# The recurrent mixer's triangular solve: 64x64 products replaced by products of the 32x32 blocks that are used

## What is computed

```python
def wkv_scan(s0, scan_in):
    def step(s, inp):
        w, kk, a, k, v, r = inp
        sa = jnp.einsum('dbhij,dbhj->dbhi', s, kk)
        s = s * w[..., None, :] - sa[..., :, None] * (kk * a)[..., None, :] + v[..., :, None] * k[..., None, :]
        return s, jnp.einsum('dbhij,dbhj->dbhi', s, r)
    return lax.scan(step, s0, scan_in)
```

## Time and profile before

| | us |
|---|---|
| median of 3 runs | 4448.5 (4442.09 to 4452.32) |
| the profiled execution | 4456.09 |
| its span | 4454.4 |
| busy in the span: PE, PEld, DVE | 3987.5, 2850.2, 2761.6 |
| busy in the span: ACT, POOL | 1455.8, 903.2 |
| granted TensorE clock, mean | 0.967 |
| the mixer's phase, from the span's start | about 2092 to 2822 |

### The profile page before, as it was taken

How to read it: one execution, slowest core, us unless ns; L and a number is a source line. 1 busy time by engine, 2 the same in 40 slices (tenths; PEclk the granted TensorE clock), 3 DMA queues, 4 the chain that set the end, 5 groups by cost and what they waited for, 6 DMA issues and landing times. The chain is left out here.

```text
span 4454.4 us, 75524 instructions
## 1 busy us (share of the span) xinstructions
PE 3987.5 (90%) x29982; PEld 2850.2 (64%) x29982; DVE 2761.6 (62%) x5967; ACT 1455.8 (33%) x3250; POOL 903.2 (20%) x926
## 2 busy tenths in 40 slices
PE   8989999988999899998999999898999777777777
PEld 6747887756788687787888888686444333333332
DVE  5674433665533476755666666235778888888885
ACT  3353342343523335712444544333111111111111
POOL 1101110110201101110000000100344444444443
PEclk9999999999999999998999999899999999999999
DMA  4203443311443310231000000434999999999998
GB/s 130 82 26 111 155 139 98 105 33 38 158 148 121 116 57 20 73 124 47 19 18 26 24 18 6 140 112 153 378 405 421 421 416 413 413 406 416 414 407 336
DMA packets 150673, 795.25 MB, mean 179 GB/s; under 512 B 19960, under 2 KB 23272, under 8 KB 83504
## 3 DMA queue, kind: packets, MB, share of 16 engines
q0 software_dynamic: 84560, 574.75, 32.0%
q1 hardware_dynamic: 58272, 188.32, 13.0%
q10 hardware_dynamic: 7488, 27.30, 1.9%
HBM read 766.11 MB, written 20.00 MB: 176 GB/s over the span
## 5 line engine op out<-in xcount | busy, mean ns | idle before, releaser
L3228 PE MATMUL psum<-rows,diag 128*128 128x512 f32 x2048 | 967.2, 620 | 260.2 <-ACT diag L3107 247.4
L3228 PEld LDWEIGHTS psum<-rows,diag 128*128 128x128 f32 x2048 | 396.1, 198 | 788.6 <-issue 775.6
L2926 POOL DMA_INDIRECT rows<-in_peer_uv,sel_idx x512 | 616.0, 1203 | 739.7 <-PE psum L3228 682.7
L2969 DVE SCALAR_TENSOR_TENSOR uh<-rows,h_rows 128x1024 f32<-128x1024 f32 x512 | 627.8, 1226 | 208.9 <-DMA rows<-in_peer_uv,sel_idx 183.1
L529 DVE TENSOR_TENSOR w_split_lo<-w_raw,w_split_hi 128x1024 fp32r<-128x1024 f32 (+1 forms) x271 | 327.2, 1218 | 496.1 <-ACT w_split_hi L516 491.4
L516 ACT CAST w_split_hi<-w_raw 128x1024 fp32r<-128x1024 f32 (+1 forms) x271 | 276.6, 1028 | 613.7 <-PE psum L465 395.0
L3100 ACT ACTIVATE g<-g 128x4 f32<-128x4 f32 x128 | 26.3, 205 | 1087.8 <-DVE g L2980 1087.8
L693 POOL TENSOR_TENSOR uT_lo<-normed_rows,uT_hi 128x512 fp32r<-128x512 f32 x64 | 90.3, 1411 | 667.0 <-ACT uT_hi L669 667.0
L465 PE MATMUL psum<-hT_mlp_hi,w_split_hi 128*128 128x512 f32 x512 | 201.7, 394 | 5.2 <-DVE hT_mlp_lo L261 5.1
L465 PE MATMUL psum<-hT_mlp_lo,w_split_hi 128*128 128x512 f32 x512 | 201.0, 393 | 0.0
L465 PE MATMUL psum<-hT_mlp_hi,w_split_lo 128*128 128x512 f32 x512 | 200.8, 392 | 0.0
(11 more groups left out here) (528 smaller groups left out, 8505.8 us busy)
## 6 DMA issues: line engine op xcount, KB each, us to landing
w_raw<-in_w_in SPq DMA_DIRECT2D x105, 512.0 KB
w_raw<-in_w_up SPq DMA_DIRECT2D x64, 512.0 KB
w_raw<-in_w_down SPq DMA_DIRECT2D x64, 512.0 KB
amask_sb<-in_w_mod ACTq DMA_DIRECT2D x48, 512.0 KB, 4.6
wq<-in_peer_wq SPq DMA_DIRECT2D x24, 512.0 KB
rows<-in_peer_uv,sel_idx POOLq DMA_INDIRECT x512
qkpad<-in_w_out SPq DMA_DIRECT2D x12, 512.0 KB, 5.5
w_raw<-in_w_out SPq DMA_DIRECT2D x12, 512.0 KB
```

Of the source, the lines that this page charges most:

```text
L2926: nc.gpsimd.indirect_dma_start(out=rows[:, n % RB, :], out_offset=None, in_=I["peer_uv"], in_offset=bass.IndirectOffsetOnAxis(ap=sel[:, t, ...
L2969: nc.vector.scalar_tensor_tensor(prod[:], rows[:, n % RB, 0:D], 1.0, h[:, t, :], ALU.mult, ALU.mult, accum_out=dots[:, (n // BATCH) % 2, s ...
L3228: last = nc.tensor.matmul(psum[:, 2 * (t % 2) + half, :], diag[:, n % (2 * BATCH), :], rows[:, n % RB, D + half * NB:D + (half + 1) * NB], ...
```

## The change

It replaces `by_head` in the 30 solve groups of each unit. Levels 1 to 4 use `by_quarter`: for each of the four quarters of the partitions, the 32x32 product of the head's diagonal block on those partitions. Level 5 uses `across`: for each head one 32x32 product, from one quarter's rows to the other quarter's output partitions. The rest of a cell's PSUM region and of U isn't written any more. All other products, waits, copies and masks are as they were.

```diff
+    quarters = tuple(slice(32 * j, 32 * j + 32) for j in range(4))
...
+    def by_quarter(out, lhsT, rhs):
+
+        for j, at in enumerate(quarters):
+            own = quarters[j % 2]
+            last = nc.tensor.matmul(out[at, own], lhsT[at, own], rhs[at, own], start=True, stop=True)
+        return last
+
+    def across(out, lhsT, rhs, source, target, mine, others):
+
+        for h in range(2):
+            rows = quarters[2 * h + source]
+            last = nc.tensor.matmul(out[quarters[2 * h + target], others], lhsT[rows, mine], rhs[rows, others],
+                                    start=True, stop=True)
         return last
...
                     for i in range(4):
                         c = 4 * b + i
-                        last = by_head(psum[:, b, i * L_CH:(i + 1) * L_CH], AT[:, c], X[:, c], True, True)
+                        out = psum[:, b, i * L_CH:(i + 1) * L_CH]
+                        if lv < LEVELS:
+                            last = by_quarter(out, AT[:, c], X[:, c])
+                        else:
+                            last = across(out, AT[:, c], X[:, c], d, 1 - d, quarters[1 - d], quarters[d])
                     last.then_inc(u_ready, 1)
...
                         y = Y[:, u % 3, c]
-                        l_, r_ = (y, U[:, c]) if lv < LEVELS else (U[:, c], y)
-                        last = by_head(psum[:, b, i * L_CH:(i + 1) * L_CH], l_, r_, True, True)
+                        out = psum[:, b, i * L_CH:(i + 1) * L_CH]
+                        if lv < LEVELS:
+                            last = by_quarter(out, y, U[:, c])
+                        else:
+                            last = across(out, U[:, c], y, 1 - d, d, quarters[d], quarters[1 - d])
                     last.then_inc(z_ready, 1)
```

## The result

The changed kernel takes 4502.35 us (median of 4, 4497.29 to 4512.57) against 4448.5 for the kernel before beside it (median of 3, 4442.09 to 4452.32): a ratio of 1.0126, interval 1.0111 to 1.014. A fourth execution of the kernel before, slow at 5680.36 us, is left out of its median. The change costs about 54 us, where 18 were forecast (4467): the sign and the range hold, the size is short by 35 us.

A forecast was written before the change was run, and what follows sets the result against it. TensorE's order of issue was taken to bound the mixer's phase. Stream and shape changes summed to +8 us (10.7 - 2.5), clock +10, together nearly +19 on the 4448.5 median: 4467 us, range 4442 to 4550.

The forecast's parts named there:

- the sign: Whole kernel: slower by over 0.2%, given 0.74; faster by over 0.2% and within it, 0.13 each.
- the range: Whole kernel: 4442 to 4550 us, with 2 in 10 left outside.
- What bounds the phase: Mixer's phase, 730 us: TensorE's order of issue sets its length, not the solve's own chain.
- The stream: Solve groups: four 32x32 products side by side take 32 ns, a group 0.254 us instead of 0.467; 102 us saved.
- The rival of four that don't start together: Solve groups: only two products stream side by side, 4565 us, or issue bounds each record, about 4725; chance 0.09 together.
- The change of shape: Between 64x64 and 32x32 groups: 0.095 us each way, plus next weights loaded in the open, 0.025 entering, 0.05 leaving.
- the W slots: Solve groups between W's products and N's, covering a wait: loss of only +0.01 us each; full loss would add 5 us.
- The longer program, "which I cost at nothing": Instruction fetch for levels 1 to 4, whose instructions double: costed at nothing, as DMA engines are 7% busy.
- the estimate of the sequencer's speed: TensorE's feed: 24 instructions shown under 8 ns each, up to 88 wanted in 0.9 us; near but enough.
- The clock: Mixer's phase: sparse stretches fall to 1.2 GHz in every second iteration, 8 more at 1.3 us, +10 us.
- The prediction's own sign of being wrong: Mixer's slices: a clock under 0.95 would show the forecast wrong.
- Iteration 0: No scan there, so solve follows solve without a change of shape from slot 12: shorter, -2.5 us taken between 0 and 4.5.

The follow-up runs named there:

- half_quarters: Changed kernel with levels 1 to 4 multiplying only quarters 0 and 2, half of the blocks left out; 4539.41 us, ratio 1.0204 to the kernel before.
- level5_only: Kernel before with only level 5 (96 of 480 solve groups) in 32x32, levels 1 to 4 unchanged; 4455.65 us, ratio 1.0009.

## Why the prediction was right, and where it was short

- **What bounds the phase** held: TensorE's order of issue. All of the change's effects were read from its starts.
- **The stream** held: four 32x32 products run side by side, 32 ns a set, and an undisturbed group of 32 matmuls takes 262 ns from first to last start. The rival of four that don't start together falls for the pitch, 8 ns for each matmul. The 25 ns per matmul of the Trainium skill, "TensorE: Matmul & The Clock Gate", Back-to-back issue gap, doesn't hold across tiles here.
- **The change of shape** held as a price, 0.10 us from start to start for 64x64 to 32x32, with the weights in the open behind it. Its sum was set too high. For units 1 to 14 it gave +9.5 us; the line through `half_quarters` leaves 14 x 0.08 = 1 (standard error 2.4). `level5_only` costs 0.10 to 0.15 us in six of its eight units at full clock and gains 0.12 and 0.17 in the other two, where the prices give 0.2 to 0.3 of loss. Perhaps more of the visits lie in front of a wait than the W slots counted; that was not tried.
- **The longer program, "which I cost at nothing"**, is the step that failed. It was argued from a DMA share of 7%, which says nothing on how fast one queue's blocks follow each other; and the estimate of the sequencer's speed (10 ns an instruction wanted, 8 shown over 24) was about a short run of instructions, not a supply over microseconds. Dry time in the phase rose by 24 us, 20 of them in units 1 to 14: where a slot wants an instruction every 10 ns, the supply gave one in about 14.
- **The clock** was the right mechanism and mis-sized: 8 stretches and 10 us expected, 62 us more of low clock found, which at 0.36 to 0.44 is 22 to 27 us. The prediction's own sign of being wrong, a clock under 0.95 in the mixer, came: 0.93. The reason given (the groups stream half as long) is not the whole of it. `half_quarters` streams as long as the changed kernel, with half of the products at work, and has twice the low clock.

For units 1 to 14 together: they are 46.2 us longer than before. 68 us more low clock x 0.36 = 24.6; dry time +20; together 44.6, leaving 1.6 for stream and shape. At 0.44 the clock has 30, and the sum is 4 us over; so the clock took 25 to 30, the supply 20, stream and shape about nothing. Iteration 0 was not shorter either (39.7 us, 39.1 before): 4.4 us more of low clock and two dry places of 0.7 and 0.8 us stand against what it saved.

The range held in part by luck. It was wide because of the clock, and some 24 of the 54 us came from the supply, which had no term in it. The phase took 776 us, outside the 740 to 755 that the prediction named. The sign rested on +8 for shape and stream, which came out near nothing, and on the clock, which was right. Dry time and low clock are not quite separate, since a dry place also lets the array rest; how many of the low stretches a dry place started stays open.

## What to carry to other kernels

Smaller tiles side by side save stream time, but each one is a weight load and a matmul to be fetched, and each interruption by another shape costs about 0.1 us on the way in and 0.12 to 0.17 on the way out. Before splitting products, count the visits between shapes and the instructions that each block of several microseconds wants, not only the time of one instruction. Look at the granted clock by stretches: in these kernels, less of the array at work went with more time at 1.2 GHz, and that took more than was left of the stream's gain.

## What the runs showed of the hardware

- TensorE's instructions come in packets of 16 KB, 256 instructions. At 88 instructions in 0.9 to 1.0 us it ran dry again and again, for 0.17 to 1.5 us at a time, always at the same place of a block of 256; where it ran dry in every block, a block took 3.5 to 3.6 us. At the kernel before's rate of at most one in 14.6 ns it didn't. A short run may be faster: groups of 32 instructions in 0.25 us (`half_quarters`, `level5_only`) brought no dry place.
- More time at 1.2 GHz went with less of the array at work in the same stream time: 102 us with four 32x32 products side by side, 217 with two, 260 with two and two of 2 columns, against 40 with 64x64 and 44 with 64x64 and visits to 32x32. These are single traces, and the kernels with 217 and 260 also hold other values.
- A us at 1.2 GHz cost 0.36 to 0.44 us here, less than the half that a stretch of nothing but streaming would lose.
- Two f32 weight loads and matmuls in 32x32 tiles of different rows and columns start 7 ns apart, and four pairs of them fit in 32 ns.
